# Five recurrence levels of a triangular inverse moved from 128x128 products to 32x32 diagonal blocks

## The reference, cut to what matters

```
def step(S, inp):
    r_t, w_t, k_t, v_t, kk_t, b_t = inp
    sa = jnp.einsum('bhvk,bhk->bhv', S, kk_t)
    S = S * w_t[:, :, None, :] - sa[..., None] * b_t[:, :, None, :] + v_t[..., None] * k_t[:, :, None, :]
    return S, jnp.einsum('bhvk,bhk->bhv', S, r_t)
```

## Time and profile before

| | |
|---|---|
| median of 3 runs | 2044.34 us |
| span of the profiled execution | 2043.6 us |
| TensorE (PE) busy in it | 1855.5 us, 91% |
| VectorE (DVE), ScalarE (ACT), GpSimd (POOL) busy | 941.1, 600.7, 364.8 us |
| recurrent stage, 8 laps | from about 472 to 1140 us of the span |

### The profile page before, as it was taken

One profiled execution on the slowest core, in us unless ns is written; L12 is line 12 of the kernel. 1 busy time (PEld: TensorE's weight loads), 2 busy tenths in 40 slices (PEclk: granted clock), 3 DMA queues, 4 the chain that ended last, 5 costly groups with the idle time before them and its releaser, 6 DMA issues. The chain is left out here.

```text
span 2043.6 us, 33681 instructions
## 1 busy us (share of the span) xinstructions
PE 1855.5 (91%) x13379; PEld 1542.9 (75%) x13379; DVE 941.1 (46%) x1522; ACT 600.7 (29%) x842; POOL 364.8 (18%) x331
## 2 busy tenths in 40 slices
PE   7999999998999999999999899999988887877776
PEld 7999999997787878877888799999967443443332
DVE  6553445547465465664755544555533121112213
ACT  5333232323233133232332533334434111100112
POOL 0640003113120321212203000273032000000002
PEclk9999999999999999999999899999988988988888
DMA  7444344434222131222220543644663999999995
GB/s 278 165 147 176 122 168 168 147 127 134 78 89 94 52 115 64 89 97 69 93 88 21 191 185 134 248 165 182 234 266 151 421 430 431 431 431 432 432 431 236
DMA packets 46599, 409.32 MB, mean 200 GB/s; under 512 B 6580, under 2 KB 8376, under 8 KB 16696
## 3 DMA queue, kind: packets, MB, share of 16 engines
q1 hardware_dynamic: 46520, 408.17, 51.5%
HBM read 396.98 MB, written 11.18 MB: 200 GB/s over the span
## 5 line engine op out<-in xcount | busy, mean ns | idle before, releaser
L380 PE MATMUL ps<-x_high,w_high 128*128 128x288 f32 x928 | 255.6, 302 | 9.7 <-ACT w_high L586 8.9
L381 PE MATMUL ps<-x_rest,w_high 128*128 128x288 f32 x928 | 251.5, 298 | 0.0
L380 PEld LDWEIGHTS ps<-x_high,w_high 128*128 128x128 f32 x928 | 175.7, 189 | 13.2 <-ACT w_high L586 10.5
L381 PEld LDWEIGHTS ps<-x_rest,w_high 128*128 128x128 f32 x928 | 175.7, 189 | 0.5
L542 ACT ACTIVATE w_high<-w_raw 128x2048 fp32r<-128x2048 f32 x57 | 109.2, 1916 | 152.6 <-DMA w_raw<-in_w_main 78.3
L1598 POOL TENSOR_TENSOR xm<-ring,const 128x512 f32<-128x512 f32 x56 | 94.9, 1694 | 306.8 <-DVE ring L1495 221.9
L1108 PE MATMUL ps<-x_high,r_high 128*128 128x288 f32 x512 | 146.1, 310 | 0.0
L653 DVE TENSOR_TENSOR w_rest<-w_raw,w_high 128x2048 fp32r<-128x2048 f32 x58 | 138.8, 2395 | 11.3 <-ACT w_high L542 11.1
L385 PE MATMUL ps<-x_high,w_rest 128*128 128x288 f32 x928 | 132.1, 295 | 1.0 <-DVE w_rest L653 1.0
L1108 PE MATMUL ps<-rx_low,r_high 128*128 128x288 f32 x480 | 130.7, 298 | 0.0
L385 PEld LDWEIGHTS ps<-x_high,w_rest 128*128 128x128 f32 x928 | 126.0, 188 | 1.2 <-DVE w_rest L653 1.2
(11 more groups left out here) (574 smaller groups left out, 4237.5 us busy)
## 6 DMA issues: line engine op xcount, KB each, us to landing
w_raw<-in_w_main SPq DMA_DIRECT2D x57, 1024.0 KB, 4.9
ring<-in_w_g SPq DMA_DIRECT2D x32, 1024.0 KB, 4.8
half_b<-in_w_egu SPq DMA_DIRECT2D x16, 2048.0 KB, 22.5
half_a<-in_w_egu SPq DMA_DIRECT2D x15, 2048.0 KB, 18.2
ring<-in_w_u SPq DMA_DIRECT2D x32, 512.0 KB, 3.5
ring<-in_w_gate SPq DMA_DIRECT2D x8, 2048.0 KB, 7.8
ring<-in_w_out SPq DMA_DIRECT2D x8, 2048.0 KB, 8.3
half_d<-in_w_egu SPq DMA_DIRECT2D x8, 2048.0 KB, 22.5
```

Source lines behind the costliest of these rows:

```text
L380: mm(o, high[:, t % 2, k, :], x_h[:, k, :], start=(k == 0), stop=False)
L381: ins = mm(o, high[:, t % 2, k, :], x_l[:, k, :], start=False, stop=False)
```

## The change

The first five levels (blocks of 1 to 16) work on the sixteen 32x32 blocks on the diagonals only: DVE copies them out of B into a compact tile `bc` of 128 x 4 x 32 (partition block n holds diagonal block n of each of the four matrices). Level one needs no product: its inverse is I minus the mask, so DVE makes it with a mask, a 32x32-wise transpose and a subtraction (`x0`, `xt`, `t0`). For the next four levels POOL makes the masks (`x1`, and `x2` for three levels at once). `forward(l)` on TensorE multiplies mask and transposed inverse in sixteen 32x32 products, one per array position (row block n, column block j), and makes the transpose of `tc` by four products of 128x32 with the identity; ACT copies both results in turn (`zc`, `uc`); `back(l)` is sixteen 32x32 products; DVE subtracts once (`updated`). Only the transposed inverse `tc` is kept up; `um` is put together at the end. The two last levels are plain block products: `z5`, `u5` for 64 and `z6`, `u6` for 128.

The same fillers stand between the new products in other portions. Sample products move to other PSUM banks, `wtmp` gets its own place, POOL clears `um` and `tm64` once before the loop, and the constants tile holds the compact masks in place of the full ones (704 of its 3304 columns go).

```diff
-                for l in LV:
-                    pe.wait_ge(g_.sem, g_.at(f"x{l}", i))
-                    pe.wait_ge(v.sem, v.at("bk11" if l == 0 else f"t{l - 1}", i))
-                    if l:
-                        pe.wait_ge(a.sem, a.at(f"z{l - 1}", i)) if l > 1 else None
-                    for j in range(4):
-                        ins = mm(ps[:, 6, j * P:(j + 1) * P], xm[:, l % 2, j, :], ident if l == 0 else tm[:, j, :],
-                    q.done(ins, f"z{l}")
...
-                    name, *parts = {1: ("G10", 18, 32, 48), 2: ("U10", 0, 2, 4), 3: ("U10", 4, 6, 8), 4: ("U11", 0, 2, 3),
-                                     5: ("U11", 3, 5, 6), 6: ("U11", 6, 8)
-                                    }.get(l, (None,))
-                    if name:
-                        filler(name, *parts[0:2])
-                    pe.wait_ge(a.sem, a.at(f"z{l}", i))
-                    pe.wait_ge(v.sem, v.at(f"u{l - 1}", i))
-                    if l < 6:
-                        for j in range(4):
-                            ins = mm(ps[:, 2, j * P:(j + 1) * P], um[:, j, :], zm[:, j, :], start=True, stop=True)
-                        q.done(ins, f"t{l}")
-                    for j in range(4):
-                        ins = mm(ps[:, 3, j * P:(j + 1) * P], zm[:, j, :], um[:, j, :], start=True, stop=True)
-                    q.done(ins, f"u{l}")
-                    if len(parts) == 3:
-                        filler(name, *parts[1:3])
...
+
+                def forward(l):
+
+                    pe.wait_ge(g_.sem, g_.at("x1" if l == 1 else "x2", i))
+                    pe.wait_ge(v.sem, v.at("sk1" if l == 1 else f"t{l - 1}", i))
+                    settled(pe)
+                    for j in range(4):
+                        for n in range(NBLK):
+                            ins = mm(ps[block_(j), 3 + n, 0:BLK], xm[block_(n), l, j, :], tc[block_(n), j, :], start=True, stop=True)
+                    q.done(ins, f"z{l}")
+                    for j in range(4):
+                        ins = mm(ps[block_(j), 2, 0:P], tc[:, j, :], ident, start=True, stop=True)
+                    q.done(ins, f"ub{l}")
+
+                def back(l):
+
+                    pe.wait_ge(a.sem, a.at(f"ub{l}", i))
+                    settled(pe)
+                    for n in range(NBLK):
+                        for j in range(4):
+                            ins = mm(ps[block_(n), 3 + j, 0:BLK], uc[block_(j), n, :], zc[block_(j), n, :], start=True, stop=True)
+                    q.done(ins, f"t{l}")
                 filler("G10", 0, 12)
+                forward(1)
+                filler("G10", 12, 22)
+                back(1)
+                pe.wait_ge(v.sem, v.at("wm1", i))
+                pe.wait_ge(g_.sem, g_.at("sx0", i))
+                sample("sz0", lambda h: sxm[:, 0, h, :], lambda h: K("ident", NSM)[:, 0:NSM])
+                filler("G10", 22, 32)
+                forward(2)
+                filler("U10", 0, 2)
+                back(2)
+                pe.wait_ge(g_.sem, g_.at("sx1", i))
+                pe.wait_ge(v.sem, v.at("st0", i))
+                sample("sz1", lambda h: sxm[:, 1, h, :], lambda h: st_[:, h, :])
+                filler("U10", 2, 4)
+                forward(3)
+                filler("U10", 4, 6)
+                back(3)
+                pe.wait_ge(a.sem, a.at("sz1", i))
+                pe.wait_ge(v.sem, v.at("w1", i))
+                sample("su1", lambda h: sz[:, h, :], lambda h: su[:, h, :])
+                filler("U10", 6, 8)
+                forward(4)
+                filler("G10", 32, 40)
+                back(4)
+                filler("G10", 40, 48)
+                pe.wait_ge(v.sem, v.at("t4", i))
+                settled(pe)
+                for j in range(4):
+                    for g in range(2):
+                        ins = mm(ps[block_(2 * g + 1), 3 + 2 * g, j * BLK:(j + 1) * BLK], bbm[block_(2 * g), j // 2, j % 2, 0, block_(2 * g + 1)],
+                                 tc[block_(2 * g), j, :], start=True, stop=True)
+                q.done(ins, "z5")
...
+                filler("U11", 0, 2)
+                settled(pe)
+                for j in range(4):
+                    mm(ps[block_(1), 4, j * BLK:(j + 1) * BLK], uc[block_(1), j, :], zc[block_(1), j, :], start=True, stop=True)
+                    for g in range(2):
+                        ins = mm(ps[block_(2 * g), 4 + 2 * g, j * BLK:(j + 1) * BLK], zc[block_(2 * g + 1), j, :], uc[block_(2 * g + 1), j, :],
                                  start=True, stop=True)
+                q.done(ins, "u5")
+                filler("U11", 2, 4)
+                for j in range(4):
+                    ins = mm(ps[64:128, 3, j * 64:(j + 1) * 64], bbm[0:64, j // 2, j % 2, 0, 64:128], tm64[0:64, j, :], start=True, stop=True)
+                q.done(ins, "z6")
+                filler("U11", 4, 6)
+                for j in range(4):
+                    ins = mm(ps[0:64, 5, j * 64:(j + 1) * 64], z6[:, j, :], um[64:128, j, 64:128], start=True, stop=True)
+                q.done(ins, "u6")
+                filler("U11", 6, 8)
...
-                for l in range(1, 7):
+                for l in range(1, 5):
                     act.wait_ge(q.sem, q.at(f"z{l}", i))
-                    act.wait_ge(q.sem, q.at(f"u{l - 1}", i)) if l > 1 else act.wait_ge(v.sem, v.at("w1", i))
-                    a.done(fn(zm, ps[:, 6, :].rearrange("p (j t) -> p j t", j=4), ACT.Copy), f"z{l}")
-                    if l == 1:
+                    if l > 1:
+                        act.wait_ge(q.sem, q.at(f"t{l - 1}", i))
+                    a.done(fn(zc, ps[:, 3:7, 0:BLK], ACT.Copy), f"z{l}")
+                    act.wait_ge(q.sem, q.at(f"ub{l}", i))
+                    a.done(fn(flat(uc), ps[:, 2, 0:P], ACT.Copy), f"ub{l}")
+                    if l == 2:
                         act.wait_ge(q.sem, q.at("sz1", i))
-                        a.done(fn(sz[:, :, :], ps[0:NSM, 4, 0:64].rearrange("p (h t) -> p h t", h=2), ACT.Copy), "sz1")
-                    if l == 2:
+                        a.done(fn(sz[:, :, :], ps[0:NSM, 7, 0:64].rearrange("p (h t) -> p h t", h=2), ACT.Copy), "sz1")
+                act.wait_ge(v.sem, v.at("t4", i))
+                fn(tm64[block_(0), :, 0:BLK], tc[block_(0), :, :], ACT.Copy)
+                a.done(fn(tm64[block_(1), :, BLK:2 * BLK], tc[block_(1), :, :], ACT.Copy), "td")
+                act.wait_ge(q.sem, q.at("z5", i))
+                fn(zc[block_(1), :, :], ps[block_(1), 3, 0:P].rearrange("p (j t) -> p j t", j=4), ACT.Copy)
+                a.done(fn(zc[block_(3), :, :], ps[block_(3), 5, 0:P].rearrange("p (j t) -> p j t", j=4), ACT.Copy), "z5")
+                act.wait_ge(v.sem, v.at("ua", i))
+                for n in reversed(range(NBLK)):
+                    ins = fn(um[block_(n), :, block_(n)], uc[block_(n), :, :], ACT.Copy)
+                a.done(ins, "ud")
+                act.wait_ge(q.sem, q.at("z6", i))
+                a.done(fn(z6, ps[64:128, 3, 0:256].rearrange("p (j t) -> p j t", j=4), ACT.Copy), "z6")
+                tanh("10")
...
+                bb = bbm[:, :, :, 0, :].rearrange("p h c t -> p (h c) t")
+                W("bk11")
+                for n in range(NBLK):
+                    ins = nc.vector.tensor_copy(bc[block_(n), :, :], bb[block_(n), :, block_(n)])
+                v.done(ins, "bc")
+                W("bc")
+                level = lambda l: K("level_c")[:, l * BLK:(l + 1) * BLK].unsqueeze(1).to_broadcast([P, 4, BLK])
+                v.done(tt(xm[:, 0, :, :], bc[:, :, :], level(0), ALU.mult), "x0")
+                W("x0")
+                v.done(nc.vector.transpose(flat(uc), flat(xm[:, 0, :, :])), "xt")
+                W("xt")
+                v.done(tt(tc, K("ident_c").unsqueeze(1).to_broadcast([P, 4, BLK]), uc, ALU.subtract), "t0")
...
+                def updated(l):
+                    WQ(f"t{l}")
+                    v.done(tt(tc, tc, ps[:, 3:7, 0:BLK], ALU.subtract), f"t{l}")
...
+                decay(0)
+                decay(1)
+                updated(1)
+                dve.wait_ge(g_.sem, g_.at("sx0", i))
+                v.done(tt(su[:, :, :], one2, sxm[:, 0, :, :], ALU.subtract), "su0")
+                WQ("sz0")
+                v.done(tt(st_[:, :, :], one2, h2(ps[0:NSM, 7, 0:64]), ALU.subtract), "st0")
+                rest("10", 0, 8)
+                rest("10", 8, 16)
+                updated(2)
+                differences("k", 9)
+                mixes("k", k, 9)
+                W("us_k")
+                v.done(ts(kk, k, par("k_k", i + 1), None, ALU.mult), "kkr")
+                updated(3)
+                WQ("su1")
+                v.done(tt(su[:, :, :], su[:, :, :], h2(ps[0:NSM, 7, 0:64]), ALU.subtract), "su1")
+                differences("r", 1)
+                mixes("r", r, 1)
+                updated(4)
+                W("t4")
+                v.done(nc.vector.transpose(flat(uc), flat(tc)), "ua")
+                scaled("10")
+                WQ("u5")
```

(45 more changed lines are left out.)

164 lines of the change are left out of this document (46 added, 118 removed).

## The result

The changed kernel takes 1955.8 us (median of four runs, 1955.15 to 1961.01) against 2043.91 for the kernel before, run beside it: a ratio of 0.9571, with an interval of 0.9558 to 0.9585. The forecast was 1968, so the gain is 88 us where 76 were expected.

A forecast was written before the change was run, and what follows sets the result against it. TensorE's work was taken to bound the rewritten stretch: 13.3 + 4.8 + 3.1 + 0.6 + 1.1 = 22.9 us against 32.39, 76 us over eight laps, 0.4 from constants, giving 1968 us; 8-in-10 range 1951 to 2012.

The forecast's parts named there:

- What bounds the stretch: From a lap's first product of the inverse to the first after it, 32.39 us: TensorE's summed work sets the time.
- Filler: Weight products between the inverse's products, 36 gate and 16 "up": unchanged, 4.9 + 8.0 us a lap, 13.3 with samples.
- Groups, changes of shape, samples: TensorE in the stretch: small-product groups 4.8 us, 28 tile-shape changes at 0.11 us 3.1, tiny sample products 0.4.
- Start of the chain: Ahead of a lap's first product of the inverse: DVE now builds the start, so it comes 0.6 us later.
- Hand-overs: Waits between TensorE and the copying engines in the stretch: mostly hidden by filler, 1.1 us a lap showing, tightest before level two.
- Range: Stretch of 21 to 27 us, giving 1950 to 1998 us at the ends, mostly 1955 to 1985.
- Constants: Load at the kernel's start: 352 KB of 1652 KB less, up to 0.8 us saved, taken as 0.4.
- hand-overs: Rival, chance 0.15: copies out of four PSUM banks cost 0.60 us, 3.2 us per lap lost beyond filler, 1994 us.
- Small products in turn: Rival, chance 0.16: 32x32 products run one after another at 0.06 us, groups take 0.96; 2016 us, or 2037.
- The clock: Rival, chance 0.04: tile groups bring TensorE's clock to half in the stretch, up to 2125 us; decides from about 19 us low.
- Nothing left at the end: Rival, chance 0.03: the expert weights' stream later gives the saved time back, 2044 us.

## Why the prediction came out as it did

*What bounds the stretch*: right. TensorE is busy for 21.28 of 21.47 us, and every edit that added work to it or a wait ahead of it lengthened the lap, by 0.40 a group, 0.13 a change, 0.93 for 0.91 us put ahead of the chain.

*Filler*: 12.9 us were taken (13.3 with the samples). At the starts in the trace, 0.1325 and 0.487, 36 and 16 products are 4.8 + 7.8 = 12.6.

*Groups, changes of shape, samples*: 4.8 + 3.1 + 0.4 = 8.3 were taken; the stretch less filler and idle time is 21.47 - 12.6 - 0.2 = 8.7. The terms were a little low together, and that this and the filler nearly cancel is luck. A group by itself is 0.28 to 0.40 to the next start with one change in it; the 64-blocks are 0.37, the 128-blocks 0.60, as taken with a change of 0.12.

*Start of the chain*: 0.6 later was taken, and the first product comes 0.25 later in the lap (24.57 us from its start instead of 24.32). DVE's last masks start at the same place of the lap in both kernels (643.64 - 624.04 = 19.60, and 663.88 - 644.27 = 19.61), and from their end to the first product it is 2.49 us where 2.84 were taken. The term had 0.12 for each hand-over, which is the price between two engines; on DVE an operation that waits for the one before starts 0.03 to 0.04 behind its end (647.07 to 647.11, 647.40 to 647.43, 647.74 to 647.78). The transpose was the operation without a row; it is 0.31, close to the 0.28 taken.

*Hand-overs*: this term was mis-sized most, 1.1 us a lap against 0.2. The tight place at level 1 was where the prediction put it, but its 0.3 did not show, and the block groups, "about even", were all covered. With the chain's 0.35 and the filler's 0.3 less and the groups' 0.4 more, the stretch comes to 21.47 + 0.25 = 21.7 from its old start instead of 22.9: 9 of the 12 us that the forecast missed. The rest lies in front of the stage and behind it, in the spread of its executions.

*Range*: its ends were worked out 2 to 3 us too low. By the same sum, 21 and 27 us for the stretch give 1953 and 2001, not 1950 and 1998; the result lies inside either way.

*Constants*: the load is 1300 KB instead of 1652, but the 0.4 us at the start cannot be seen; starts between 8.95 and 10.18 us in thirteen profiles hide it.

*Rivals*: hand-overs, refuted by copies of 0.28 in place of 0.60. Small products in turn, refuted by rows of 32 records in 0.36 and a price of 0.40 for a repeated group; the rule of 62 ns a matmul without hardware decoding (the Trainium skill, TensorE: Matmul & The Clock Gate, "Wait — 56ns, not 53.3ns?") would make that 16 x 0.062 = 1.0, so it does not set the price here. The clock, right not to be the forecast, but nearer than its 0.04 and the 19 us of low clock suggest: at 1.00 in the changed kernel's laps, it fell in every lap with a wait of 4.5 us at the jump, and in every stretch with seven waits of 0.1 to 1.1 us. Nothing left at the end, refuted: behind the stage the program took no longer than before (912.3, 917.4).

## What to carry to other kernels

Where one engine sets the pace and fillers hide the rest, sum its work, and ask of every wait that you close which other engine's place is next; closing the first one gave nothing in two runs, and 7 to 8 us once the second was moved too. Small tiles cut the work but multiply TensorE's instructions: count a loop's instructions before and after, since past some length here each lap loaded its code again, and the clock fell in that wait too. Put products of one shape side by side: each change cost 0.13 us.

## What was not expected of the hardware

- A loop of 1588 rows of PE is kept, one of 1844 is loaded anew in each lap (9 packets of 16 KB), at 4.4 to 4.8 us a jump; the changed kernel is not far from that edge (the kernel before had 1194).
- A wait of TensorE of 1.8 us was followed by a fall of the clock to half in three of eight laps, 3.4 us long; one of 4.4 to 4.9 us by one of 3.4 or 6.8 us in every lap.
- Thirty-two small records behind filler start within 0.17 us, but the same group repeated takes 0.39 to 0.40: the first burst is not the steady rate.
- A mask on DVE took 0.57 instead of 0.29 while POOL made one, and POOL's took 0.57 instead of 0.46 where DVE was first, in every lap; the one that began 0.04 us later was the slower one, so the two seem to hinder each other.
